# Attention items of 384 and 512 keys: the gate and the reciprocal move from a VectorE pass over the probabilities into the matrix that TensorE multiplies them by

## The chip, the cores and the metric

One NeuronCore of a Trainium2 chip runs the whole program. The metric is the device time of one execution in microseconds (us); lower is better. PE is TensorE (PEld its weight loads), DVE is VectorE, ACT is ScalarE, POOL is GpSimd, SP is SyncE.

## The reference, cut to what matters

The reference is a stack of three transformer-like blocks over 512 tokens with a model width of 1024: a gated delta net, retention, and a third block whose mixer joins an HGRN2 branch and a sparse attention (`nsa`). Each is followed by a convolutional feed-forward layer. The change touches only the last softmax part of `nsa`. It has 8 query heads of 64 channels in 2 key/value groups of 4, and three branches: over 31 compressed blocks, over selected blocks of 64 keys, and over a window of 512 keys. With 512 tokens there are only 8 blocks to select from and 16 may be selected, and the window holds every key, so that the second and third branches are both causal softmax attention over all keys, with keys and values of their own:

```
sw = einsum('bgrnqd,bgnkd->bgrnqk', qw, kwin) * scale
pw = softmax(where(mw, sw, NEG), axis=-1)
o_win = einsum('bgrnqk,bgnkd->bgrnqd', pw, vwin)
...
gates = sigmoid(g_pre)
o = gates[..., 0:1] * o_cmp + gates[..., 1:2] * o_slc + gates[..., 2:3] * o_win
```

Everything is float32.

## The kernel before, in words

The program keeps activations transposed in SBUF (channels on partitions, 512 tokens along the free axis), streams weights through a ring of three slots on SP's DMA queue, and goes through its stages one after the other. Each engine has an instruction stream written out by hand, with one semaphore per engine that counts its finished steps. A wait names the step of another engine (`at("dve", "nsa", "p", n, g)`) and an engine runs its instructions strictly in the order in which they are written.

The attention stage is `pe_nsa`, `act_nsa` and `dve_nsa`. After a part that normalizes, rotates and compresses, it loops over 36 items (`ITEMS`, L1877): for r in 0 to 3 (the head within its group) first one item of branch 0 (b = 0, compressed keys, all 512 queries at once), then for b = 1 and b = 2 four items (b, i) with i = 0 to 3. Item (b, i) holds the 128 queries of block i against the keys 0 to 128 (i + 1), and both groups g = 0 and 1. So an item with i = 2 has 384 keys and one with i = 3 has 512. `Pn` has three buffers for probabilities (queries on partitions, keys along the free axis), `PTn` two for their transposes. Banks 0, 1, 6 and 7 of PSUM hold the scores of two items, banks 2 and 3 the transposes of the two groups, banks 4 and 5 collect the output.

An item n goes through these steps.

- `scores(n)`, PE, L1942 (L1938 for b = 0): queries by keys, into a score bank. It waits until the exponentials of item n − 2 have read that bank.
- `front(n)`, DVE, L2090: adds the causal mask and finds the row maximum, in one custom instruction for each group (L2079, L2082 and L2085 for b = 0).
- `exp(n)`, ACT, L2013 (L2007 for b = 0): the exponential into `Pn`, with the row sum in `small`.
- DVE, L2113: the reciprocal of both row sums. Then L2117, one instruction for each group: the item's probabilities, in place, times reciprocal times gate; this is step "p" of (n, g). For b = 0 the lines are L2102 to L2109.
- PE, L1972: a transpose of each 128x128 block of the scaled probabilities into bank 2 + g, after step "p" of the group and after ACT's copy of the item before has read the bank.
- ACT, L2028 (L2026 for b = 0): the copy of the transposed block row from the bank to `PTn`.
- `values(n)`, PE, L1958 (L1954 for b = 0): values by transposed probabilities, added up in banks 4 and 5 over the branches. As reciprocal and gate are in the probabilities, the branches need no further scaling.

The order in each engine is what couples the items. For item n, PE does `scores(n + 2)`, the transposes of n, `values(n - 1)`. DVE does `front(n + 1)`, then waits for `exp(n)`, then the reciprocal and L2117 of n. ACT does `exp(n + 1)`, then the copies of n. In the first (b = 1) item of each r but the first, DVE also copies the finished output of r − 1 out of banks 4 and 5 into `HT` (L2136, L2137). After the last item it does so for r = 3, and the next stage's products (L267) follow.

Neither DMA nor POOL has a part in this loop. The matrix `ident` (128x128 identity) is the operand of all transposes in the program. Elsewhere, the first block's chunk code has, for each of 8 heads, four transposes of 128x128 at L996 and four plain products of 128x128 by 128 columns at L1001; four more at L1067 stream `ident` as the moving operand.

Of the kernel before, what the change touches and what calls it, by code (L numbers as in the profile page):

```python
# [12 lines left out]
P = 128  # L13
# [73 lines left out]
def program(nc, dr, out, plan):  # L87
# [3 lines left out]
    with ExitStack() as ctx:  # L91
# [7 lines left out]
        B4 = [b[:, :].rearrange("p (i c) -> p i c", c=P) for b in B]  # L99
# [22 lines left out]
        ident = sb("ident", [P, P])  # L122
# [15 lines left out]
        small = sb("small", [P, 64])  # L138
# [3 lines left out]
        def region(offset, *shape):  # L142
            size = int(np.prod(shape))
            v = arena[:, offset:offset + size]
            if len(shape) == 2:
                v = v.rearrange("p (a b) -> p a b", b=shape[1])
            if len(shape) == 3:
                v = v.rearrange("p (a b c) -> p a b c", b=shape[1], c=shape[2])
            return v
# [757 lines left out]
        o = 0  # L907
        OT_g = region(0, GH, T)
        o = GH * T
# [399 lines left out]
        o = 16 * T  # L1309
# [174 lines left out]
        o = 0  # L1484
# [6 lines left out]
        VSW = region(o, NT, 280); o += NT * 280  # L1491
# [370 lines left out]
        o = 4 * CB * NCMP  # L1862
# [3 lines left out]
        o = work  # L1866
        Pn = [region(o + m * 2 * T, 2 * NT, P) for m in range(3)]; o += 6 * T
# [1 line left out]
        tri = region(o, T); o += T  # L1869
        KCMP = region(o, 32); o += 32  # L1870
        VCMP = region(o, 2, ND); o += 2 * ND
        assert o <= 26000
        SB = ((0, 1), (6, 7))
        NORMED = [4, 0, 1, 2, 3, 6, 7]
        GAIN = {0: 0, 1: 0, 2: 0, 3: 0, 4: 1, 6: 2, 7: 3}
# [6 lines left out]
        def pe_nsa(pe):  # L1882
# [29 lines left out]
            for kv in (1, 0):  # L1912
                pe.wait_ge(act_done, at("act", "nsa", "silu", kv))
                for hc in range(2):
                    last = nc.tensor.transpose(B[6][:, (2 * kv + hc) * 2 * NCMP:(2 * kv + hc + 1) * 2 * NCMP],
                                               SIL[0:2 * NCMP, kv, hc * P:(hc + 1) * P], ident[0:2 * NCMP, 0:2 * NCMP])
# [3 lines left out]
            for g in range(NG):  # L1920
# [3 lines left out]
                for hc in range(2):  # L1924
                    last = nc.tensor.matmul(B[3][0:NCMP, g * ND:(g + 1) * ND], HID[:, 2 + hc, blk], w2c[:, 1, hc, :],
                                            start=(hc == 0), stop=(hc == 1))
# [37 lines left out]
            for n, (r, b, i) in enumerate(ITEMS):  # L1964
                if n + 2 < len(ITEMS):
                    scores(n + 2)
                for g in range(NG):
                    pe.wait_ge(dve_done, at("dve", "nsa", "p", n, g))
                    if n:
                        pe.wait_ge(act_done, at("act", "nsa", "pt", n - 1, g))  # L1970
                    for j in range(NT if b == 0 else i + 1):
                        last = nc.tensor.transpose(B4[2 + g][:, j, :], Pn[n % 3][:, 4 * g + j, :], ident[:, :])  # L1972
                    last.then_inc(pe_done, PE.tick("nsa", "pt", n, g))
                if n:
                    values(n - 1)
# [56 lines left out]
        def dve_nsa(dve):  # L2032
            begin(dve, "dve", "nsa")

            def step(ins):

                ins.then_inc(dve_done, DV.tick())
                dve.wait_ge(dve_done, DV.n)

            def blocks_of(kv):  # L2040
                for g in range(NG):
                    for a in range(2):

                        tok = NX[half(g), 4 + kv, a * CS:a * CS + NCMP * CS].rearrange("p (n l) -> p l n", l=CS)
                        dst = XP[half(g), kv, a * CS:(a + 1) * CS, g * NCMP:(g + 1) * NCMP]
                        pos = pecmp[half(g), kv, a * CS:(a + 1) * CS].rearrange("p (l o) -> p l o", o=1).to_broadcast([ND, CS, NCMP])
                        ins = nc.vector.tensor_tensor(dst, tok, pos, ALU.add)  # L2047
                ins.then_inc(dve_done, DV.tick("nsa", "blocks", kv))

            blocks_of(1)  # L2050
            for n, c in enumerate(NORMED):
                dve.wait_ge(act_done, at("act", "nsa", "std", n))
                nc.vector.scalar_tensor_tensor(out=NX[:, c, :], in0=NX[:, c, :], scalar=gvec[:, 8 + GAIN[c]:9 + GAIN[c]], in1=rsn[n % 2],
                                               op0=ALU.mult, op1=ALU.mult).then_inc(dve_done, DV.tick("nsa", "normed", n))
                dve.wait_ge(pe_done, at("pe", "nsa", "rot", n))
                nc.vector.tensor_tensor(tan, B[2 + n % 2][:, :], SINF, ALU.mult).then_inc(dve_done, DV.tick())
                step(nc.vector.tensor_tensor(NX[:, c, :], NX[:, c, :], COSF, ALU.mult))
                nc.vector.tensor_tensor(NX[:, c, :], NX[:, c, :], tan, ALU.add).then_inc(dve_done, DV.tick("nsa", "rotated", n))
                dve.wait_ge(dve_done, DV.n)
                if c == 4:  # L2060
                    blocks_of(0)
            for m in range(3):

                nc.vector.memset(Pn[m][:, :, :], 0.0).then_inc(dve_done, DV.tick())
            nc.vector.memset(tri, 0.0).then_inc(dve_done, DV.tick())
            dve.wait_ge(dve_done, DV.n)
            step(nc.vector.tensor_copy(tri[:, 3 * P:4 * P], causal[:, 2, :]))
            cm = cmask[:, :, 0:NCMP]
            valid = cmask[:, :, 31:32].rearrange("p i o -> p (i o)")

            def front(n):

                r, b, i = ITEMS[n]
                dve.wait_ge(pe_done, at("pe", "nsa", "score", n))
                if b == 0:
                    S = [B4[SB[n % 2][g]][:, :, 0:NCMP] for g in range(NG)]
                    m4 = [small[:, 24 + 4 * g:28 + 4 * g] for g in range(NG)]
                    for g in range(NG):
                        ins = nc.vector.tensor_tensor(S[g], S[g], cm, ALU.add)  # L2079
                    step(ins)  # L2080
                    for g in range(NG):
                        ins = nc.vector.reduce_max(m4[g], S[g], AX)  # L2082
                    step(ins)
                    for g in range(NG):
                        nc.vector.tensor_tensor(S[g], S[g], m4[g].rearrange("p (i o) -> p i o", o=1).to_broadcast([P, NT, NCMP]), ALU.subtract)\  # L2085
                            .then_inc(dve_done, DV.tick("nsa", "max", n, g))
                else:
                    for g in range(NG):
                        S, c = B[SB[n % 2][g]], 2 * (n % 2) + g
                        nc.vector.tensor_tensor_reduce(out=S[:, 0:(i + 1) * P], in0=S[:, 0:(i + 1) * P], in1=tri[:, (3 - i) * P:4 * P],  # L2090
                                                       scale=-SCALE, scalar=3e38, op0=ALU.add, op1=ALU.min,
                                                       accum_out=small[:, 20 + c:21 + c]).then_inc(dve_done, DV.tick("nsa", "max", n, g))

            front(0)
            for n, (r, b, i) in enumerate(ITEMS):
                if n + 1 < len(ITEMS):
                    front(n + 1)
                dve.wait_ge(act_done, at("act", "nsa", "exp", n, 1))
                if b == 0:
                    Pc = Pn[n % 3][:, :, 0:NCMP]  # L2100
                    s8 = small[:, 32:40]
                    step(nc.vector.reduce_sum(s8, Pc, AX))  # L2102
                    step(nc.vector.reciprocal(s8, s8))
                    for g in range(NG):
                        s4 = s8[:, 4 * g:4 * g + 4]
                        step(nc.vector.tensor_tensor(s4, s4, valid, ALU.mult))
                        step(nc.vector.tensor_tensor(s4, s4, VSW[:, :, 256 + 3 * (NG * 2 * g + r)], ALU.mult))
                        w4 = s4.rearrange("p (i o) -> p i o", o=1).to_broadcast([P, NT, NCMP])
                        nc.vector.tensor_tensor(Pc[:, 4 * g:4 * g + 4, :], Pc[:, 4 * g:4 * g + 4, :], w4, ALU.mult)\  # L2109
                            .then_inc(dve_done, DV.tick("nsa", "p", n, g))  # L2110
                else:
                    c = 40 + 2 * (n % 2)
                    step(nc.vector.reciprocal(small[:, c:c + 2], small[:, c:c + 2]))  # L2113
                    for g in range(NG):
                        head = NG * 2 * g + r
                        p = Pn[n % 3][:, 4 * g:4 * g + i + 1, :].rearrange("p j c -> p (j c)")
                        nc.vector.tensor_scalar(p, p, small[:, c + g:c + g + 1], VSW[:, i, 256 + 3 * head + b:257 + 3 * head + b],  # L2117
                                                ALU.mult, ALU.mult).then_inc(dve_done, DV.tick("nsa", "p", n, g))
                if b == 1 and i == 0 and r:
                    dve_o(dve, r - 1)  # L2120
            dve_o(dve, 3)
            DV.mark("end", "nsa")
# [357 lines left out]
```

## Time and profile before

| what | value |
|---|---|
| median of 3 runs | 3007.68 us (3004.35 to 3011.74) |
| the profiled execution's own time | 3000.66 us |
| its span, first to last instruction | 2998.6 us, 29328 instructions |
| PE busy | 2813.1 us, 94% |
| DVE busy | 1547.3 us, 52% |
| ACT busy | 640.8 us, 21% |
| POOL busy | 149.6 us, 5% |
| mean granted TensorE clock | 0.969 of full speed |

A busy time is the union of an engine's instructions; records of PE overlap each other, since matmuls are pipelined. A line number is that of the kernel's source, so all instructions of a program line fall into a group. The "idle before" of a group is the time its engine had nothing to do just before the group's instructions, and the arrow names what ended it. The attention loop described above runs from about 2437 to 2530 us of the span.

### The profile page before, as it was taken

The page shows a single profiled execution, that of the slowest core. Times are in us where ns is not written, and L with a number is a line of the kernel's source. Part 1 is how long each engine was busy: PE and PEld are TensorE (multiplying, and loading weights), DVE is VectorE, ACT ScalarE, POOL GpSimd, SP SyncE. Part 2 cuts the span into 40 slices and gives each one's busy share as a digit, 9 for nine tenths or more (in the row PEclk, how much of TensorE's full clock was granted, in tenths as well). Part 3 has the DMA queues.
Part 4 walks back from the last instruction along what each step waited for, and adds up shares of the span by engine and source line. Part 5 has one row for each costly group of instructions (what it writes and reads, how often), then busy time and mean ns, then how long its engine had stood idle before and what let it go on. Part 6 is the DMA issues. An engine that isn't in the chain of part 4 may idle for free. (4 is left out here: it accounts for less than half of the span.)

```text
span 2998.6 us, 29328 instructions
## 1 busy us (share of the span) xinstructions
PE 2813.1 (94%) x11724; PEld 1964.9 (66%) x11724; DVE 1547.3 (52%) x2740; ACT 640.8 (21%) x1124; POOL 149.6 (5%) x118
## 2 busy tenths in 40 slices
PE   6999999988999999999989899999699899999999
PEld 5566666656888884444434688888245445588888
DVE  4555555546777542112211677764646566566652
ACT  0211122102111002111110211100635465222200
POOL 0000000001000001000000100000122200000000
PEclk9999999899999999999989999999899999999999
DMA  7111121112444331111112244433011130222121
GB/s 306 39 57 56 60 91 75 57 41 85 164 166 157 149 124 65 58 60 60 65 51 84 84 169 165 155 134 123 32 56 44 57 113 1 82 88 85 67 97 48
DMA packets 24486, 274.95 MB, mean 92 GB/s; under 512 B 3480, under 2 KB 4376, under 8 KB 7072
## 3 DMA queue, kind: packets, MB, share of 16 engines
q1 hardware_dynamic: 19440, 266.45, 24.0%
q10 hardware_dynamic: 4912, 6.63, 0.7%
q8 instruction: 94, 1.54, 0.2%
q14 instruction: 40, 0.33, 0.0%
HBM read 270.97 MB, written 2.10 MB: 91 GB/s over the span
## 5 line engine op out<-in xcount | busy, mean ns | idle before, releaser
L323 PE MATMUL bank<-HT,ring 128*128 128x256 f32 x1056 | 256.6, 388 | 21.0 <-ACT HT L671 12.7
L939 PE MATMUL bank<-HT,ring 128*128 128x512 f32 x512 | 261.0, 640 | 0.0
L323 PE MATMUL bank<-arena 128*128 128x256 f32 x1056 | 249.5, 379 | 0.0
L323 PE MATMUL bank<-arena,ring 128*128 128x256 f32 x1056 | 249.5, 379 | 0.0
L323 PEld LDWEIGHTS bank<-HT,ring 128*128 128x128 f32 x1056 | 203.3, 194 | 52.2 <-issue 24.2
L323 PEld LDWEIGHTS bank<-arena 128*128 128x128 f32 x1056 | 200.6, 190 | 27.3
L323 PEld LDWEIGHTS bank<-arena,ring 128*128 128x128 f32 x1056 | 200.6, 190 | 27.3
L400 PE MATMUL bank<-arena,ring 128*128 128x256 f32 x936 | 207.5, 380 | 5.7 <-ACT arena L470 3.8
L267 PE MATMUL bank<-arena,ring 128*128 128x512 f32 x448 | 199.8, 606 | 11.0 <-issue 9.6
L400 PEld LDWEIGHTS bank<-arena,ring 128*128 128x128 f32 x936 | 177.0, 190 | 31.1 <-ACT arena L470 5.1
L244 DVE SCALAR_TENSOR_TENSOR arena<-ring,evec,arena 128x512 f32<-128x512 f32 x224 | 167.3, 747 | 3.8
L267 PEld LDWEIGHTS bank<-arena,ring 128*128 128x128 f32 x448 | 87.0, 195 | 122.1 <-issue 122.1
L860 ACT ACTIVATE arena<-bank,ffc 128x512 f32<-128x512 f32 x66 | 51.3, 777 | 471.3 <-DVE bank L788 471.3
L1535 PE MATMUL bank<-HT,ring 128*128 128x512 f32 x320 | 147.6, 598 | 4.3 <-ACT HT L699 4.3
L939 PEld LDWEIGHTS bank<-HT,ring 128*128 128x128 f32 x512 | 95.4, 205 | 79.1 <-issue 79.1
L323 PE MATMUL bank<-HT,arena 128*128 128x256 f32 x528 | 126.5, 382 | 0.9 <-DVE arena L838 0.8
L1355 PE MATMUL bank<-ring,HT 128*128 128x512 f32 x256 | 114.7, 608 | 8.2 <-ACT arena L660 8.2
L1336 PE MATMUL bank<-HT,ring 128*128 128x512 f32 x256 | 113.6, 605 | 6.3 <-ACT HT L671 6.3
L400 PE MATMUL bank<-arena 128*128 128x256 f32 x528 | 116.4, 379 | 0.0
L323 PEld LDWEIGHTS bank<-HT,arena 128*128 128x128 f32 x528 | 98.6, 190 | 19.3 <-DVE arena L838 6.5
L1369 PE MATMUL bank<-HT,ring 128*128 128x512 f32 x256 | 110.5, 592 | 0.0
L605 DVE SCALAR_TENSOR_TENSOR XT<-bank,mod,XT 128x512 f32<-128x512 f32 x24 | 18.0, 751 | 178.3 <-PE bank L267 178.3
(396 smaller groups left out, 4014.2 us busy)
## 6 DMA issues: line engine op xcount, KB each, us to landing
ring<-w_ada SPq DMA_DIRECT2D x33, 2048.0 KB, 8.0
ring<-w_up SPq DMA_DIRECT2D x33, 2048.0 KB, 7.8
ring<-w_down SPq DMA_DIRECT2D x24, 1408.0 KB, 6.0
ring<-w_gdn SPq DMA_DIRECT2D x8, 2048.0 KB, 12.4
ring<-w_ret_qk SPq DMA_DIRECT2D x4, 2048.0 KB, 7.9
ring<-w_ret_v SPq DMA_DIRECT2D x4, 2048.0 KB, 7.8
ring<-w_ret_g SPq DMA_DIRECT2D x4, 2048.0 KB, 7.9
ring<-w_ret_out SPq DMA_DIRECT2D x4, 2048.0 KB, 7.8
```

The lines of the kernel that those rows point to most:

```text
L244: ins = nc.vector.scalar_tensor_tensor(out=acc, in0=w[:, :, k, :], scalar=evec[:, e, k:k + 1], in1=acc, op0=ALU.mult, op1=ALU.add)
L267: last = nc.tensor.matmul(bank[:, :], w[:, n % per_load, k, :], src(k), start=(k == 0), stop=(k == kc - 1))
L323: last = nc.tensor.matmul(out_, w[:, k, :], x[:, k, :], start=(first and k == 0), stop=(k == 3), skip_group_check=not first)
L400: last = nc.tensor.matmul(out_, w[:, k, :], x(k), start=(first and k == 0), stop=(k == KH2 - 1), skip_group_check=not first)
L605: nc.vector.scalar_tensor_tensor(out=XT[:, n, :], in0=B[n % 2][:, :], scalar=g[:, i, gate + n:gate + n + 1], in1=XT[:, n, :], op0=ALU.mult ...
L860: nc.scalar.activation(ffn_y[:, j % 2, :], B[j % 2][:, :], ACT.Identity, scale=ffc[:, i, j, 0, 2:3], bias=ffc[:, i, j, 0, 3:4])\
L939: last = nc.tensor.matmul(B[u % 2][:, :], w[:, u, k, :], HT[:, k, :], start=(k == 0), stop=(k == KC - 1))
L1336: last = nc.tensor.matmul(B[X + u][:, :], w[:, u, k, :], HT[:, k, :], start=(k == 0), stop=(k == KC - 1))
L1355: last = nc.tensor.matmul(B[Y + i][:, :], HT[:, k, i * P:(i + 1) * P], w[:, k, :], start=(k == 0), stop=(k == KC - 1))
L1369: last = nc.tensor.matmul(B[Y + u][:, :], w[:, u, k, :], HT[:, k, :], start=(k == 0), stop=(k == KC - 1))
L1535: last = nc.tensor.matmul(bank[:, :], w[:, u, k, :], HT[:, k, :], start=(k == 0), stop=(k == KC - 1))
```

## The change

In items of 384 and 512 keys (b > 0, i >= 2) L2117 no longer multiplies the probabilities. It multiplies the identity by reciprocal and gate, which gives a diagonal matrix of 128x128, into one of six new buffers `scale_n` (three items by two groups). PE then multiplies each block of the unscaled probabilities by this diagonal, with a plain `matmul` in place of the `transpose` with the identity. The result is the same scaled, transposed block in the same bank. The other items (b = 0 and i < 2) stay as they were. Waits and semaphore steps stay the same, and so does the number of instructions in the program's text.

```
         VCMP = region(o, 2, ND); o += 2 * ND
-        assert o <= 26000
+        scale_n = [region(o + m * P, P) for m in range(6)]; o += 6 * P
+        assert o <= 26000, o
...
                     for j in range(NT if b == 0 else i + 1):
-                        last = nc.tensor.transpose(B4[2 + g][:, j, :], Pn[n % 3][:, 4 * g + j, :], ident[:, :])
+                        if b == 0 or i < 2:
+                            last = nc.tensor.transpose(B4[2 + g][:, j, :], Pn[n % 3][:, 4 * g + j, :], ident[:, :])
+                        else:
+                            last = nc.tensor.matmul(B4[2 + g][:, j, :], Pn[n % 3][:, 4 * g + j, :], scale_n[2 * (n % 3) + g], start=True, stop=True)
                     last.then_inc(pe_done, PE.tick("nsa", "pt", n, g))
...
                     for g in range(NG):
                         head = NG * 2 * g + r
-                        p = Pn[n % 3][:, 4 * g:4 * g + i + 1, :].rearrange("p j c -> p (j c)")
-                        nc.vector.tensor_scalar(p, p, small[:, c + g:c + g + 1], VSW[:, i, 256 + 3 * head + b:257 + 3 * head + b],
+                        if i < 2:
+                            p = q = Pn[n % 3][:, 4 * g:4 * g + i + 1, :].rearrange("p j c -> p (j c)")
+                        else:
+                            p, q = scale_n[2 * (n % 3) + g], ident[:, :]
+                        nc.vector.tensor_scalar(p, q, small[:, c + g:c + g + 1], VSW[:, i, 256 + 3 * head + b:257 + 3 * head + b],
                                                 ALU.mult, ALU.mult).then_inc(dve_done, DV.tick("nsa", "p", n, g))
```

## Rows read from the trace of the kernel before

**Rows 1.** The page's busy line of PE, whole span: busy us, share, instructions.

```profile
PE 2813.1 (94%) x11724; PEld 1964.9 (66%) x11724; DVE 1547.3 (52%) x2740; ACT 640.8 (21%) x1124; POOL 149.6 (5%) x118
```

**Rows 2.** Windows, the attention loop: length, busy us (instructions) of each engine, clock, DMA.

```profile
2437.00:2530.00 93.00, 83.90 (x704) 52.01 (x705) 74.00 (x283) 63.82 (x208) 0.00 (x0) 0.98 0.01 1
```

**Rows 3.** Waits from 2437 to 2530: who for whom, us in total, times, longest.

```profile
ACT arena L2028 <- PE bank L1972: 18.4, 31, 1.1
...
PE bank L1972 <- DVE arena L2117: 5.3, 8, 1.1
```

**Rows 4.** Timeline around item (1, 2) of r = 2: start, us, engine, line, idle.

```profile
2487.72 1.13 PE L1942 MATMUL bank<-arena 64*128 64x512 f32 x4
...
2490.36 0.87 DVE L2117 TENSOR_SCALAR arena<-arena,small 128x384 f32<-128x384 f32 x2
...
2490.89 0.94 PE L1972 MATMUL bank<-ident,arena 128*128 128x128 f32 x6 [0.67 <-DVE arena L2117]
```

**Rows 5.** Timeline around items (2, 2) and (2, 3) of r = 1; last row: r = 2.

```profile
2476.90 1.08 PE L1938 MATMUL bank<-arena 64*128 64x31 f32 x16
...
2477.53 0.87 DVE L2117 TENSOR_SCALAR arena<-arena,small 128x384 f32<-128x384 f32 x2
...
2478.06 0.94 PE L1972 MATMUL bank<-ident,arena 128*128 128x128 f32 x6
...
2478.31 0.48 DVE L2079 TENSOR_TENSOR bank<-bank,cmask 128x124 f32<-128x124 f32 x2
...
2479.93 1.00 DVE L2117 TENSOR_SCALAR arena<-arena,small 128x512 f32<-128x512 f32 x2
...
2480.53 1.11 PE L1972 MATMUL bank<-ident,arena 128*128 128x128 f32 x8 [0.52 <-DVE arena L2117]
...
2502.69 1.11 PE L1972 MATMUL bank<-ident,arena 128*128 128x128 f32 x8 [0.52 <-DVE arena L2117]
```

**Rows 6.** Timeline, the last two items of the loop (r = 3).

```profile
2522.39 0.93 PE L1972 MATMUL bank<-ident,arena 128*128 128x128 f32 x6 [1.10 <-DVE arena L2117]
...
2523.85 1.09 PE L1972 MATMUL bank<-ident,arena 128*128 128x128 f32 x8
2524.60 1.09 ACT L2028 ACTIVATE arena<-bank 128x512 f32<-128x512 f32 x2 [0.69 <-PE bank L1972]
...
2524.87 1.96 PE L1958 MATMUL bank<-arena 128*64 128x128 f32 x28
```

**Rows 7.** Lines L996, L1001 and L1067: records, ns min/median/max, first and last start.

```profile
L996 PEld LDWEIGHTS bank<-ident,arena x32: 140/141/144, 115.7 to 599.3; 128*128 128x128 f32 x32
L996 PE MATMUL bank<-ident,arena x32: 272/273/273, 115.8 to 599.4; 128*128 128x128 f32 x32
...
L1001 PEld LDWEIGHTS bank<-arena x64: 186/192/193, 116.3 to 600.4; 128*128 128x128 f32 x64
L1001 PE MATMUL bank<-arena x64: 275/275/348, 116.4 to 600.5; 128*128 128x128 f32 x64
...
L1067 PE MATMUL bank<-ident,rqk x64: 275/275/561, 170.6 to 638.6; 128*128 128x128 f32 x64
```

**Rows 8.** Timeline of PE, a batch of plain 128x128 products (L1014, first block).

```profile
125.59 1.05 PE L1014 MATMUL bank<-arena 128*128 128x128 f32 x8
```

**Rows 9.** Timeline, the transposes of item (1, 0) of r = 2.

```profile
2485.90 0.44 PE L1972 MATMUL bank<-ident,arena 128*128 128x128 f32 x2
```

**Rows 10.** Lines by form, L2117: count, busy us, mean ns, idle before.

```profile
L2117 DVE TENSOR_SCALAR arena<-arena,small 128x512 f32<-128x512 f32 x16 | 8.0, 544 | 0.3
L2117 DVE TENSOR_SCALAR arena<-arena,small 128x384 f32<-128x384 f32 x16 | 6.9, 476 | 0.3
L2117 DVE TENSOR_SCALAR arena<-arena,small 128x128 f32<-128x128 f32 x16 | 4.8, 344 | 0.3
```

**Rows 11.** Timeline: the copies of item (1, 3), r = 2, and PE's reading.

```profile
2493.74 1.08 ACT L2028 ACTIVATE arena<-bank 128x512 f32<-128x512 f32 x2 [0.63 <-PE bank L1972]
...
2496.03 1.09 PE L1958 MATMUL bank<-arena 128*64 128x128 f32 x16
```

## The prediction

> **What bounds the kernel now.** The busy line of the page first [rows 1]: TensorE (PE) is busy for 94% of the span. That is a mean over stages, so the second view is the one of windows, for the attention loop alone (2437 to 2530 us) [rows 2]: PE is busy 83.9 of 93.0 us, VectorE (DVE) 74.0, ScalarE (ACT) 63.8. PE has 9 us to spare there, and the third view, the waits [rows 3], says where: 5.3 us in 8 waits of the transposes at L1972 for the DVE multiplication at L2117; the rest lies at the loop's two ends and in crumbs. So the loop is PE's, save for two places in each of the four rounds (a round is the nine items of one r).
>
> The timeline shows both. **Place A**, item (1, 2), 384 keys [rows 4]: PE ends scores of 512 columns at 2488.85; DVE can reduce these scores (L2090) only then, before the reciprocal and L2117, which starts at 2490.36 and releases the transposes at 2490.89. PE had 0.67 us of nothing. **Place B**, item (2, 3), 512 keys [rows 5]: after L2117 of item (2, 2) DVE makes the next round's front (from L2079 at 2478.31), then the reciprocal, and L2117 at 2479.93 releases PE at 2480.53, after 0.52 us of nothing. Between these places PE's instructions stand end to end. In the last round B has no next front before it, so that its 512-key item waits for nothing, and its 384-key item (2, 2) waits 1.10 us in the manner of A [rows 6]. That makes 4 + 3 + 1 = 8 waits.
>
> **What the change costs PE.** The items of 384 and 512 keys have 3 and 4 blocks for each of 2 groups: 6 and 8 products, twice in each round, 4 × 2 × 14 = 112 in all. A transpose is one record: L996 has 8 heads × 4 = 32 in the program and 32 in the trace. A plain fp32 product of the same shape, L1001, also 8 × 4 in the program, has 64 records [rows 7]: two passes each. L1067, with the identity streamed as the changed line streams a diagonal, has 64 for its 32 too. Eight plain records in a row last 1.05 us [rows 8] and one lasts 0.275 [rows 7], so they start (1.05 − 0.275) / 7 = 0.111 us apart. Eight transposes in two groups last 1.09 us [rows 6], two in two groups 0.44 [rows 9]: six more in 0.65 us, 0.108 each. So a product costs 2 × 0.111 − 0.108 = 0.113 us more. All 112: **12.7 us** of added PE time; an item of 384 keys gets 0.68 us, one of 512 keys 0.90.
>
> The nearest rows bound this price. Below: one record after all, nothing more. Above: if the longer weight load (0.192 against 0.141 us, L1001 and L996 [rows 7]) stood in the open for both records, 2 × 0.05 = 0.10 more, 0.213 in all and 24 us for the 112. L1001's loads are no less long, and the eight records of L1014, which are of the same shape, still start 0.111 apart, so I take 0.113.
>
> **A rule against this change.** What the trace has is one record against two, 0.108 against 0.222 us [rows 7, 8]. The Trainium skill (TensorE: Matmul & The Clock Gate, section Terms) says of the transpose mode that it is "4× faster for FP32". The rows here give a factor of two. By the rule each product would cost 3 × 0.108 = 0.32 us more, 36 us in all; this is an estimate from that page, taken up below as a rival.
>
> **What it gives DVE.** L2117 shrinks from 384 or 512 columns to 128: 0.476 and 0.544 us to 0.344 [rows 10]. Two for each item, that is 0.26 and 0.40 us less, and 8 × 0.66 = 5.3 us of DVE's time. Only what stands ahead of PE's eight waits can be had back. The wait of A ends with the first L2117 alone: 0.476 − 0.344 = 0.13 us. B's has a pair of 384 before the front and one L2117 of 512: 0.26 + 0.20 = 0.46 us. Instructions, semaphores and their order stay as they are; nothing is added to ACT or to a DMA queue. The exponentials (L2013) still end before L2117 starts and are not made earlier. The copies by ACT (L2028) start later with the products that they wait for; the products by V that read them (L1958) are those of the item before, one PE turn later, and have 1.2 us of room even for 512 keys: the copies end at 2494.82, PE reads them at 2496.03 [rows 11]. That cover is whole for all items except the last of the loop.
>
> **The sum, place by place.** A, four times: PE starts 0.13 us earlier and works 0.68 longer: +0.55. Item (1, 3) behind it, four times: PE arrives later than DVE already, all of it counts: +0.90. B, three times: item (2, 2) starts at 2478.06, PE having ended at 2477.98, so it can gain 0.08 only, and takes 0.68 more: +0.60. This eats B's idle 0.52 [rows 5]; DVE's release moves from 2480.53 to 2480.07, so PE is now the late one, and item (2, 3) starts 0.08 us later. Then its own +0.90. That makes 0.98. Three rounds: 3 × (0.55 + 0.90 + 0.98) = 7.3 us. Last round: A 0.55, (1, 3) 0.90, (2, 2) 0.55 (1.10 us wait for DVE, shortened by 0.13), and the end. There PE does the products by V of (2, 2), 12 records from 2524.87 on, and then the 16 of (2, 3), which wait for ACT's copies, done at 2525.69; all end at 2526.83 [rows 6]. Twelve of 28 records in 1.96 us are 0.84, so (2, 2) is through at 2525.71. With 0.90 us more the transposing products, which ended at 2524.94, end at 2525.84 and the second copy (half of the 1.09 us) some 0.6 later, while PE gets through with (2, 2) at 2526.61: +0.75 by the one, +0.90 by the other, I take 0.85. DVE's two copies into HT (L2136, L2137) and the next stage hang on that. Last round 2.85. Together **10.1 us slower**.
>
> The profiled execution took 3000.66 us (span 2998.6 and 2.1 around it). That is 7.0 below the median of the runs, 3007.68, and 3.7 below the lowest, 3004.35. Its durations make the difference of 10.1; I put it on the median: 3007.68 + 10.1 = **3017.8 us**, a factor of 1.0034. A measurement of this kernel can tell about 0.3% from no change, 9.0 us, and the forecast lies just over it.
>
> **Rivals.**
> *One record each.* The diagonal's products might go at the transposes' pace, so that only DVE's gain is left: 4 × 0.13 + 3 × 0.46 + 0.13 = 2.0 us faster, 3005.7. The point from which it decides: a round's A and B give 0.13 + 0.46 = 0.59 us and have 28 products, so below 0.59 / 28 = 0.021 us more for a product the change doesn't lose. L1001 and L1067 speak against it with two records for each. 3%.
> *More cover than I see.* The longer turns of PE let DVE and ACT run ahead, and the crumbs of idle time go as well as B's: 12.7 less all 5.3 us of the eight waits, 7.4 us, 3015.1, and within 0.3%. Against it: at A PE waits for a chain that begins with its own scores, so A's 0.67 us can't be eaten. 12%.
> *Nothing covered.* Behind longer turns ACT's copies or an exponential come late, and B's 0.52 us is only moved: 12.7 us and no gain, 3020.4. For it: ACT waits 18.4 us in 31 waits for L1972 [rows 3], so it follows PE closely; against it, the room of 1.2 us above. 10%.
> *Four times.* A pace of 0.43 us for a product: 112 × 0.32 = 36 us, less DVE's 0.65 at A and what B covers, some 2.5 in all: 33 us, 3041. The page's estimate above is what this would be. The 64 records of L1001 speak against it. 2%.
> *The forecast*, 73%.
>
> Within the forecast the bound at 9.0 us is 1.1 us away, and the scatter of the runs shown is ±3.7: 6 in 10 of it fall above, the others within. Slower 0.44 + 0.09 + 0.02 + a little of the second rival, 0.58; faster 0.02, for the first rival's 2.0 us are themselves within 0.3%; the rest, 0.40, within. The range takes in 7.4 and 12.7 us with some 3 us of scatter on either side: 3011.5 to 3023.5.
>
> **What would show it.** In the changed trace L1972 has 80 records of transposes and 224 of plain products, weight loads near 0.19 us; its busy time is up by 12 to 13 us. A batch for 512 keys is 16 records in about 2.0 us. L2117 has only rows of 128 and 256 columns, 48 of 128. A round takes 22.16 us now (2502.69 less 2480.53 [rows 5]) and should take 24.6 (22.16 + 2.43). A's wait should be 0.54 us, B's none. The loop should end 10 us later and every other stage be as it was. The forecast is wrong if L1972 has 192 records, if a wait for ACT's copies or its exponentials stands before a PE batch in this loop, or if B still waits.

## The result, and the profile after

The changed kernel took 3011.33 us (median of 20 runs, 3005.49 to 3015.79) against 3005.12 (20 runs, 3001.65 to 3013.89): a ratio of **1.0018, 95% interval 1.0011 to 1.0024**, 5.4 us slower (3.3 to 7.2); the two medians are 6.2 us apart. The forecast was 10.1 us, a ratio of 1.0034, with 3017.8 us and a range that began at 3011.5. The direction was right, the size was not, and the median fell just below the range. The base was off too: the forecast added to 3007.68 us, the median of three runs, and twenty runs of the kernel before have 3005.12. The profiled execution took 3006.45 us, 5.8 above that of before. All figures here are of fast executions; two slow ones of the fifth set, of 4608.9 and 4921.8 us at mean clocks of 0.60 and 0.57, are left out.

The loop itself did what was forecast. It is measured from one end to the other by two PE instructions that both kernels have: the first product by V of branch 0 in round 0 (L1954, now L1955), and the first product of the next stage (L267). Timeline, before:

```profile
2442.38 1.07 PE L1954 MATMUL bank<-arena 31*64 31x512 f32 x4
...
2528.48 3.67 PE L267 MATMUL bank<-arena,ring 128*128 128x512 f32 x8 [1.65 <-issue]
```

and after:

```profile
2437.73 1.07 PE L1955 MATMUL bank<-arena 31*64 31x512 f32 x4
...
2533.83 3.67 PE L267 MATMUL bank<-arena,ring 128*128 128x512 f32 x8 [1.65 <-issue]
```

That is 86.10 us before and 96.10 after: **+10.0 us**. But the loop begins 4.65 us earlier, after 2.4 ms of a program that the change doesn't touch. From L267 to the end of the span it is 470.1 us before and 470.6 after. So in this pair of traces 4.65 of the 10.0 are missing ahead of the loop.

Windows of just this stretch, before and then after (columns as in [rows 2]):

```profile
2442.38:2528.48 86.10, 77.75 (x683) 48.42 (x683) 70.03 (x263) 60.58 (x197) 0.00 (x0) 1.00 0.01 2
```

```profile
2437.73:2533.83 96.10, 90.23 (x795) 62.88 (x795) 65.35 (x263) 62.04 (x196) 0.00 (x0) 1.00 0.01 2
```

PE has 112 records more and 12.5 us more busy time, DVE 4.7 us less; PE's idle time goes from 8.35 to 5.87 us. The clock is at its full 2.4 GHz level in both.

Lines by form of after, for [rows 10] and L1972:

```profile
L1976 PE MATMUL bank<-arena 128*128 128x128 f32 x224 | 29.3, 282 | 3.1 <-DVE arena L2124 3.1
L1976 PEld LDWEIGHTS bank<-arena 128*128 128x128 f32 x224 | 26.2, 191 | 6.2 <-DVE arena L2124 4.1 <-issue 1.5
...
L2124 DVE TENSOR_SCALAR arena<-ident,small,arena 128x128 f32<-128x128 f32 x32 | 9.6, 344 | 0.6
```

The 112 products are 224 records, as L1001 said. Their weight loads take 191 ns, and 16 records still take 2.05 us, so that the loads are hidden. PE's waits for DVE's scaling went from 5.3 us in 8 to 3.1 in 5. This is place A of after, in the round of [rows 4], and then place B, in the round of [rows 5]:

```profile
2487.82 1.13 PE L1943 MATMUL bank<-arena 64*128 64x512 f32 x4
...
2490.46 0.60 DVE L2124 TENSOR_SCALAR arena<-ident,small,arena 128x128 f32<-128x128 f32 x2
...
2490.86 1.60 PE L1976 MATMUL bank<-arena 128*128 128x128 f32 x12 [0.54 <-DVE arena L2124]
```

```profile
2476.12 1.08 PE L1939 MATMUL bank<-arena 64*128 64x31 f32 x16
...
2477.15 1.60 PE L1976 MATMUL bank<-arena 128*128 128x128 f32 x12
...
2478.88 0.60 DVE L2124 TENSOR_SCALAR arena<-ident,small,arena 128x128 f32<-128x128 f32 x2
...
2479.27 0.49 PE L1943 MATMUL bank<-arena 64*128 64x128 f32 x4
2479.69 2.05 PE L1976 MATMUL bank<-arena 128*128 128x128 f32 x16
```

A keeps a wait of 0.54 us (0.67 less 0.13). At B there is none: DVE has made both diagonals by 2479.48, PE arrives at 2479.69. A batch for 512 keys is 16 records in 2.05 us.

### The profile page after: what moved, and what is told of

It reads as the page before. It is cut to its first block and busy times, and to the rows that moved or that the text cites. A ratio compares the mean times of both kernels' runs of the same rounds, so it can differ in the third digit from the quotient of the medians.

```text
span 3004.4 us, 29552 instructions
## 1 busy us (share of the span) xinstructions
PE 2830.0 (94%) x11836; PEld 1988.9 (66%) x11836; DVE 1543.0 (51%) x2740; ACT 642.4 (21%) x1124; POOL 149.6 (5%) x118
## 5 line engine op out<-in xcount | busy, mean ns | idle before, releaser
L323 PE MATMUL bank<-HT,ring 128*128 128x256 f32 x1056 | 258.0, 390 | 20.0 <-ACT HT L671 12.7
L323 PEld LDWEIGHTS bank<-arena 128*128 128x128 f32 x1056 | 200.6, 190 | 27.3
L267 PE MATMUL bank<-arena,ring 128*128 128x512 f32 x448 | 198.5, 603 | 11.0 <-issue 9.6
L267 PEld LDWEIGHTS bank<-arena,ring 128*128 128x128 f32 x448 | 86.6, 194 | 121.4 <-issue 121.4
L1535 PE MATMUL bank<-HT,ring 128*128 128x512 f32 x320 | 148.7, 602 | 4.3 <-ACT HT L699 4.3
L1336 PE MATMUL bank<-HT,ring 128*128 128x512 f32 x256 | 113.5, 605 | 6.3 <-ACT HT L671 6.3
L400 PEld LDWEIGHTS bank<-arena 128*128 128x128 f32 x528 | 100.3, 190 | 13.6
```

The costliest lines, as they stand in the source:

```text
L267: last = nc.tensor.matmul(bank[:, :], w[:, n % per_load, k, :], src(k), start=(k == 0), stop=(k == kc - 1))
L323: last = nc.tensor.matmul(out_, w[:, k, :], x[:, k, :], start=(first and k == 0), stop=(k == 3), skip_group_check=not first)
L400: last = nc.tensor.matmul(out_, w[:, k, :], x(k), start=(first and k == 0), stop=(k == KH2 - 1), skip_group_check=not first)
L1336: last = nc.tensor.matmul(B[X + u][:, :], w[:, u, k, :], HT[:, k, :], start=(k == 0), stop=(k == KC - 1))
L1535: last = nc.tensor.matmul(bank[:, :], w[:, u, k, :], HT[:, k, :], start=(k == 0), stop=(k == KC - 1))
```

## The experiments

The question became where the missing 4 to 5 us are. There were three theories: **loop plus scatter** (the change costs its 10.0, and the first set of timings drew low), **outside** (something in the changed program makes the rest shorter in every execution), **cheaper product** (executions other than the traced ones pay less for a plain product). The kernels below also test the pieces of the sum. "Loop" is always the stretch defined above. A number of us behind a ratio is the ratio's part of the time of before in that set. Timings taken together, against the same runs of the kernel before, are called a set; the first set is the result above.

### Second set: the change taken apart

**null**, the kernel before with the buffers named and unused:

```
+        scale_n = [region(o + m * P, P) for m in range(6)]; o += 6 * P
```

> The kernel before with the six new buffers named but not used: its instructions are those of before. All theories: loop 86.1 us from the first products by V of branch 0 in round 0 to the first product of the next stage, as before, and a ratio of 1.000. What is wanted is the scatter: if two equal programs come out more than 2 us apart, the 5.4 us measured for the change (with 10.0 in the loop of the two traces) can be scatter; if they stay within 1 us, something outside the loop or in unprofiled runs has to explain the other 4.6 us.

Loop 86.11 us, ratio 1.0001 (0.9991 to 1.0010), +0.3 us. The medians, however, are 2.4 us apart the other way (3002.15 against 3004.58), so this set alone doesn't decide between scatter and a cause outside the loop.

**pe_alone**, only PE's part:

```
-                        last = nc.tensor.transpose(B4[2 + g][:, j, :], Pn[n % 3][:, 4 * g + j, :], ident[:, :])
+                        if b == 0 or i < 2:
+                            last = nc.tensor.transpose(...)
+                        else:
+                            last = nc.tensor.matmul(B4[2 + g][:, j, :], Pn[n % 3][:, 4 * g + j, :], ident[:, :], start=True, stop=True)
```

> Only PE's part: items of 384 and 512 keys are multiplied by the identity with a plain product, DVE still scales 384 and 512 columns. Theory 'loop': 224 records, A 4 x (0.68 + 0.90), B 3 x (0.09 + 0.90) since its idle 0.52 covers most of the 0.68, last items 0.68 + 0.85, in all +10.8 us in the loop and +10.8 in the median. Theory 'outside': +10.8 in the loop, and the median is some 4.6 us short of it, +6, as for the change. Theory 'cheaper unprofiled': half of it in the median, +5.4, and in the change-and-double kernel too.

Loop 97.17 us, +11.1; ratio 1.0035 (1.0022 to 1.0047), +10.5 us. Nearly all of the loop's time arrives in the whole here (6.6 to 14.1 by the interval), which speaks against a product that is cheaper by half.

**dve_alone**, only DVE's part (reciprocal and gate are left out of the items' results):

```
-                        if b == 0 or i < 2:
-                            last = nc.tensor.transpose(...)
-                        else:
-                            last = nc.tensor.matmul(..., scale_n[2 * (n % 3) + g], start=True, stop=True)
+                        last = nc.tensor.transpose(...)
```

(against the changed kernel)

> Only DVE's part: the diagonals are made (128 columns), but PE transposes the probabilities of these items with the identity as before, so reciprocal and gate are left out of their result. Theory 'loop': A 4 x -0.13, B 3 x -0.46, last -0.13: -2.0 us in the loop and in the median. Theory 'outside': -2.0 in the loop, -6 to -7 in the median. Theory 'cheaper unprofiled': -1 to -2.

Loop 83.68 us, −2.4; ratio 0.9990 (0.9981 to 0.9999), −3.0 us. The extra 4.6 us that "outside" asks for are not there. The parts are −2.4 and +11.1, together +8.7, where the change has +10.0: B's idle time is used once, either by DVE's gain or by PE's longer item.

**twice**, each diagonal product issued twice:

```
+                            nc.tensor.matmul(B4[2 + g][:, j, :], Pn[n % 3][:, 4 * g + j, :], scale_n[2 * (n % 3) + g], start=True, stop=True)
                             last = nc.tensor.matmul(B4[2 + g][:, j, :], Pn[n % 3][:, 4 * g + j, :], scale_n[2 * (n % 3) + g], start=True, stop=True)
```

> The changed kernel with each of the 112 diagonal products issued twice: 224 more records at 0.111 us. Theory 'loop': 96.1 + 24.9 = 121 us of loop, +35 us in the median against before. Theory 'outside': +35 in the loop, +30 in the median. Theory 'cheaper unprofiled' (a plain record costs half of what the trace shows): about +18 in the median.

Loop 121.13 us. The 112 added products cost 25.03, 0.2235 each, which is the forecast's 2 × 0.111. Ratio 1.0105 (1.0091 to 1.0119), +31.6 us of the 35.0 in the loop. That is far from 18; the gap of 3.4 has an interval of ±4, so it is not clear of nothing.

### Third set: the change again, one part more, and two changes of order

**after2**, the changed kernel.

> The changed kernel again, on this chip. Its own trace has the loop 10.0 us longer and the part before the loop 4.7 us shorter than before's, though that part is the same program. If the 4.7 us is scatter of single executions: loop 96.1 again, the part before the loop anywhere within 2449 to 2456, and over this set of runs a ratio between 1.0025 and 1.004. If something in the changed program lowers the rest in every execution: loop 96.1, ratio 1.0015 to 1.002 again.

Loop 96.11, ratio 1.0031 (1.0019 to 1.0043), +9.3 us. In this set nothing is clearly missing. Its part before the loop ends at 2437.46 us. (The expectations count that part from some 11 us before the first instruction: the 2442.38 of before is 2453.7 there, and the 2437.73 of after 2449.0. Counted so, `after2` has 2448.7, just under the 2449 to 2456 that were named.)

**all_diag**, the diagonal for all items with b > 0:

```
-                        if b == 0 or i < 2:
+                        if b == 0:
...
-                        if i < 2:
+                        if b == 0:
```

> The diagonal for every item with b > 0, so for 128 and 256 keys too: 48 more products, 5.4 us of PE time. In the loop: in rounds 0 to 2 the 0.45 of item (1, 1) goes into A's wait of 0.54, item (2, 1) pays 0.45 and the two of 128 keys 0.23 each; in the last round (2, 1) too is covered, by a wait of 0.96. Loop 96.1 + 3.2 = 99.3 us. Theory 'loop plus scatter': median 13.2 above before. Theory 'outside': 8.6 to 9 above.

Loop 98.64 us, 2.5 more than the change where 3.2 were expected; ratio 1.0049 (1.0037 to 1.0061), +14.7 us. For the shorter items the sum was 0.7 us too high: PE's waits for L2124 went from 3.1 us in 5 to 0.5 in 1, so that more of the added 5.4 us was covered than the 2.2 of the sum. Nothing is won by it.

**early_after**, the changed kernel with DVE's order changed for items (1, 2), (2, 2) and (2, 3) of each round, so at A, at B and at one item that doesn't wait:

```
+                early = b and (i == 2 or (b, i) == (2, 3))
-                if n + 1 < len(ITEMS):
+                if n + 1 < len(ITEMS) and not early:
                     front(n + 1)
...
+                if n + 1 < len(ITEMS) and early:
+                    front(n + 1)
```

(the second after the reciprocal and the scaling of n)

> The changed kernel with DVE's order changed at A and B: reciprocal and diagonal of item n ahead of the front of n + 1. A's wait of 0.54 goes, four times, the last 0.96 too, of which 0.3 comes back before the last item: loop 96.1 - 2.8 = 93.3 us. If the later front delays the exponentials of the 512-key item by more than PE's longer turn covers, a new wait for L2124 stands before the item of 512 keys and the loop gains less than 1 us.

Loop 92.81 us, −3.3 against the change. No wait of PE for L2124 is left in the loop. This is its PE timeline at A, with no idle time printed:

```profile
2486.99 0.49 PE L1943 MATMUL bank<-arena 64*128 64x128 f32 x4
2487.41 1.60 PE L1976 MATMUL bank<-arena 128*128 128x128 f32 x12
```

Ratio 1.0023 (1.0013 to 1.0033), +6.9 us for +6.7 in the loop.

**values_first**, the kernel before with PE's order changed for the same three items of each round, so in the last round for (2, 3) too, which did not wait:

```
+                first = b and (i == 2 or (b, i) == (2, 3))
+                if first:
+                    values(n - 1)
                 for g in range(NG):
                     pe.wait_ge(dve_done, at("dve", "nsa", "p", n, g))
...
-                if n:
+                if n and not first:
                     values(n - 1)
```

> The kernel before, with PE's order changed at A and B alone: the products by V of item n - 1 ahead of the transposes of n, so that they fill the wait for DVE. 8 waits, of which 4 x 0.59, 3 x 0.52 and 0.59 are filled: loop 86.1 - 4.5 = 81.6 us, ratio 0.9985. If PE's waits there are not what the loop's time hangs on, or DVE's next front comes late in turn, the loop stays within 1 us of 86.1.

This was a miss: loop 84.45 us, −1.65 instead of −4.5; ratio 0.9998 (0.9989 to 1.0007). This is a line of its waits (who for whom, us in total, times, longest), and then the timeline at B:

```profile
PE bank L1958 <- ACT arena L2031: 2.5, 6, 0.8
```

```profile
2492.50 0.88 PE L1958 MATMUL bank<-arena 128*64 128x128 f32 x12 [0.27 <-ACT arena L2031]
...
2495.17 0.42 PEld L1975 LDWEIGHTS bank<-ident,arena 128*128 128x128 f32 x4 [0.54 <-DVE arena L2112]
2495.17 1.26 PE L1975 MATMUL bank<-ident,arena 128*128 128x128 f32 x8
```

PE's 5.3 us of waits for the scaling became 0.2, but the products by V now come early enough to wait for ACT's copies themselves: 2.5 us in 6 waits that the kernel before doesn't have. Three of them are the 0.27 us at B; the other three, 0.22, 0.63 and 0.80 us, are in the last round, where they and the 0.21 for DVE are more than the 1.10 us that was to be filled. And now that PE is early, the next round's branch-0 item, which has the longest chain on DVE, holds it up: its eight transposes last 1.26 us in place of 1.09, the length of any eight before ([rows 6]), with a gap for L2112 between the groups. So most of what was filled came back as other waits.

### Fourth set: scatter, and a better order

**after3** and **after4** are the changed kernel, **null2** the instructions of before.

> The changed kernel a third time. Its loop has been 96.10 and 96.11 us against 86.10 and 86.11. Theory 'loop plus scatter': this set's ratio lies between 1.0025 and 1.004, since the first set's 1.0018 drew low and the second's was 1.0031. Theory 'outside': 1.0015 to 1.002. A ratio between the two leaves it open.

> The changed kernel a fourth time, a copy of the third, so that the spread between two equal kernels of one set is seen: theory 'loop plus scatter' as for the third, and the two within 3 us of each other. The part before the loop of the two traces within 2445 to 2456 us, not at one value.

> The instructions of the kernel before again: loop 86.1, ratio within 0.999 and 1.001; the part before the loop somewhere within 2445 to 2456 us, which no theory of the loop touches.

Loops 96.11, 96.11 and 86.11 us. Ratios 1.0032 (1.0019 to 1.0044), 1.0032 (1.0019 to 1.0045) and 1.0007 (0.9998 to 1.0016). Counted as in the expectations, the part before the loop ends at 2451.4, 2450.6 and 2458.0 us; the last, of the unchanged instructions, lies above the 2445 to 2456 that were named.

**combo**, the kernel before with PE's order changed at A and the last round's second wait, and DVE's at B:

```
+                first = i == 2 and (b == 1 or r == 3)
...
+                early = (b, i) == (2, 3)
```

(with the lines of `values_first` and `early_after` that use them)

> The kernel before with two changes of order: at A, and in the last round at its second wait, PE does the products by V of the item before ahead of the transposes (0.59 us of the wait filled each time); at B DVE makes reciprocal and scaling of the 512-key item ahead of the next round's front (0.52 us of wait gone). Loop 86.1 - 5 x 0.59 - 3 x 0.5 = 81.6 us. If the front of the next round comes late for it, a wait for L2112 stands before its branch-0 transposes and the loop keeps 83.1.

Loop 83.96 us, −2.1; ratio **0.9987 (0.9978 to 0.9996)**, −3.9 us. The second outcome that was named came, though by less (83.1 was said), with a wait of 0.48 us for the branch-0 scaling:

```profile
2476.61 1.09 PE L1975 MATMUL bank<-ident,arena 128*128 128x128 f32 x8
2477.63 0.88 PE L1958 MATMUL bank<-arena 128*64 128x128 f32 x12
2478.44 0.70 PE L1942 MATMUL bank<-arena 64*128 64x256 f32 x4
2479.62 1.25 PE L1975 MATMUL bank<-ident,arena 128*128 128x128 f32 x8 [0.48 <-DVE arena L2113]
```

B's 512-key item now starts right after the scores, and what was won there is lost two batches later. What is left is what was won at A and in the last round.

### Fifth set: the theories against each other

> The changed kernel in a further set. Loop 96.1. Theory 'loop plus scatter': ratio 1.0025 to 1.004, as in the two sets before (1.0031, 1.0032, 1.0032). Theory 'outside': 1.0015 to 1.002, as in the first set.

> A copy of the same, for more executions in this set: as above; both theories have its part before the loop vary by some us from trace to trace, and only 'outside' has it lie 4 to 5 us below that of the unchanged instructions in the same set.

> The unchanged instructions, in the same set: ratio 0.999 to 1.001, loop 86.1. Its part before the loop is compared with those of the two changed kernels of this set: equal within the scatter of 2.5 us by 'loop plus scatter', 4 to 5 us longer by 'outside'.

The loops take 96.09, 96.08 and 86.09 us, and yet the ratios are 1.0006 (0.9996 to 1.0016), 1.0008 (0.9996 to 1.0019) and 0.9993 (0.9983 to 1.0003): +1.8, +2.4 and −2.1 us. So "loop plus scatter" fails in its simple form: seven or eight microseconds are missing in this set, beyond the intervals, and the unchanged instructions of `null3` came out low too. In the traces of this set nothing is missing: the loop begins at 2439.34 us in null3, at 2440.50 in after5 and 2439.29 in after6.

> The two changes of order once more: loop 83.96 as before, 2.1 us under 86.1, so a ratio of 0.9993 by the loop alone; 0.9987 was measured. If the order gives what the loop shows and no more, this set lies at 0.9990 to 0.9996.

**combo2**: loop 83.91, ratio 0.9988 (0.9978 to 0.9997), a second time below 1, just under the 0.9990 to 0.9996 that were expected. That is −3.6 us, 1.4 more than the loop gives (2.2); against `null3` of the same set, −2.1, it is only 1.5 faster.

### Sixth set: does the gap grow with the products?

**four**, each diagonal product issued four times (two more lines like that of `twice`), and **after7**, the changed kernel.

> The changed kernel with each diagonal product issued four times: 672 records more than the changed kernel. Loop 96.1 + 3 x 25.0 = 171 us, 85.0 above before. The doubled kernel had 35.0 more in the loop and 31.5 in the mean of its executions; the changed one 10.0 and between 2 and 9.6. If executions other than the traced ones pay some tenth less for a plain product, the gap grows with the products: 75 to 78 in the median. If the gap is between loadings of a program and has nothing to do with the products, it stays within 0 to 8 us: 77 to 85, and most likely 81 to 84.

> The changed kernel in one more set. Loop 96.1. Sets so far: 1.0018, 1.0031, 1.0032 and 1.0006. If sets differ by the loading of the program, this one lies anywhere between 1.000 and 1.0035; a value near 1.0033 is what the loop alone gives.

**four**: loop 171.14 us, +85.0; ratio 1.0283 (1.0268 to 1.0298), +85 us (80.4 to 89.4). The 75 to 78 of a product that is a tenth cheaper in executions other than the traced ones lie outside this interval, and "cheaper product" falls; a gap that doesn't grow with the products, of up to 4.6 us, would still fit. **after7**: loop 96.10, ratio 1.0024 (1.0015 to 1.0034), +7.2 us.

## Why the prediction was right or wrong

**The price of a product: right.** Forecast 0.222 us for two records. Measured 0.2235 in `twice` (25.03 / 112) and 0.2233 in `four` ((171.14 − 96.10) / 336). By the Trainium skill's "4× faster for FP32" for the transpose mode (TensorE: Matmul & The Clock Gate, section Terms) it would be 0.43, an estimate from that page. The runs disagree and decide: they give a factor of 2.07 over the 0.108 of a transpose.

**The loop, place by place: right.** A round grew from 22.16 to 24.54 us, 2.38 where the sum had 2.43. From the last round's first product by V of branch 0 to L267 it grew by 2.88 (19.60 to 22.48), where the sum had 2.85. A's wait went to 0.54 and the last round's from 1.10 to 0.96 as forecast:

```profile
2526.23 1.60 PE L1976 MATMUL bank<-arena 128*128 128x128 f32 x12 [0.96 <-DVE arena L2124]
...
2528.35 2.05 PE L1976 MATMUL bank<-arena 128*128 128x128 f32 x16
...
2530.33 1.85 PE L1959 MATMUL bank<-arena 128*64 128x128 f32 x28
```

At B PE was to reach the 512-key item 0.08 us later; counted from the branch-0 scores (3.63 us from L1938 to L1972 in [rows 5], 3.57 from L1939 to L1976 above) it is 0.06 earlier. A batch for 512 keys in turn adds 0.96 us rather than 0.90 from its start to that of the next batch (1.02 in [rows 6], 1.98 here), twice in a round. The two errors nearly cancel. The 28 records at the end, 1.96 us before [rows 6], now run through in 1.85 without the wait for ACT. The prediction's signs came as named (80 transposes, 224 plain records, a round of 24.54 us, B without a wait) save one that it had read wrongly: it took any wait for ACT's copies before a PE batch for a sign of error, and said that between A and B PE's instructions stand end to end. There is such a wait, of 0.37 us, before the first products by V of branch 0 in rounds 1 to 3, and it is in both kernels alike (in round 2 at 2486.71 us of before and at 2486.81 of after), so that it changes nothing in the difference.

**The step that failed** is the one that put the difference of the loop on the median: "Its durations make the difference of 10.1; I put it on the median". It has two parts, and both failed. The base, 3007.68 us, is the median of three runs, and twenty runs gave 3005.12: 2.6 of the 6.5 us by which 3017.8 was missed. On the base of 3005.12 the same sum gives 3015.2 and a range from about 3009, which holds the 3011.33. The difference takes the 2.9 ms outside the loop to be the same in both kernels, in the mean of a set: the other 3.9 us. What the sets showed (the means are of each set's executions, of before and then of the kernel named):

| kernel | loop against 86.1 | whole, us against before (interval) | mean of before | mean of the kernel |
|---|---|---|---|---|
| first set | +10.0 | +5.4 (3.3 to 7.2) | 3005.7 | 3011.2 |
| after2 | +10.0 | +9.3 (5.7 to 12.9) | 3001.7 | 3010.3 |
| after3, after4 | +10.0, +10.0 | +9.6, +9.6 (5.7 to 13.5) | 3000.8 | 3010.1, 3010.1 |
| after5, after6 | +10.0, +10.0 | +1.8, +2.4 (−1.2 to 5.7) | 3006.6 | 3008.6, 3010.0 |
| after7 | +10.0 | +7.2 (4.5 to 10.2) | 3001.8 | 3009.1 |
| null, null2, null3 | 0.0, 0.0, 0.0 | +0.3, +2.1, −2.1 | 3004.4, 3000.8, 3006.6 | 3004.0, 3002.3, 3005.1 |

The whole is always less than the loop, by 0.4 to 8.2 us; the plain mean of the seven is +6.5. The changed kernel's own mean hardly moved (3008.6 to 3011.2); that of the kernel before did (3000.8 to 3006.6), and where it was high the difference is small. The loop's part repeats to 0.04 us. The rest doesn't repeat: the same program up to the loop arrives there at very different times. In two traces of one kernel, combo and combo2, the loop's first product (L1954) starts at 2440.07 and at 2449.08 us.

Over the seven traces of the changed kernel this start lies between 2437.46 and 2442.01 us, mean 2439.6; over the four of the unchanged instructions between 2439.34 and 2446.36, mean 2442.1. The difference of 2.6 us has the sign of what is missing and three quarters of its mean size, but combo's two traces alone are 9 us apart. The other kernels have the same instructions up to the loop, and `four`, built on the changed kernel, begins it at 2446.63, `values_first` at 2434.56. Over all twenty traces the twelve with the plain products have a mean of 2440.3 and the eight without 2442.2: 1.8 us, with single traces 14.5 apart.

**What is settled and what stays open.** Settled: the change costs 10.0 us where it acts, and executions other than the traced ones pay for its products too (`four`). Open: whether the rest of the changed kernel is really some 3.5 us shorter in the mean, or whether seven measurements in five sets drew low. Kernels of equal instructions differed by up to 2.1 us from the kernel before in a set, while the difference of the changed one ranged over 7.8. Most of that range comes from the kernel before's own mean, which moved by 5.8 from set to set. Against the copies of the unchanged instructions in the same set the means differ by 7.8 (`after3` and `after4` against `null2`) and by 4.2 (`after5` and `after6` against `null3`). Nothing was found in the program that would explain a shorter rest: up to the loop the instructions are the same. Two rivals were not tested by themselves. One is how a program was loaded for a set, named in an expectation. The other is the chip: the sets of `after2` and `after7` ran on one, that of `after3` on a second and that of `after5` on a third, and the smallest differences and the slowest mean of the kernel before are those of the third. For the first set the chip is not on record, and one chip alone had that mean at 3004.4, 3001.7 and 3001.8 in three sets.

**The rivals.** "One record each" fell with the 224 records, "four times" with 0.2235 us for a product. "More cover than I see" named 7.4 us and "nothing covered" 12.7; both are refused by the loop's 10.0, though the whole of the first set lay below the first of them. The forecast's own split, 6 in 10 above 0.3% and the rest within, was for scatter of the runs shown. It had no allowance for a base from three runs or for offsets between sets, and the range's lower end, some 3 us of scatter below 7.4, was too near. That the result lies only 0.2 us outside the range is no merit of the number: a smaller difference and a lower base added up.

## What to carry to other kernels

An fp32 transpose on TensorE is one record and a plain fp32 product of the same shape two: folding a scale into the transposing matrix doubles PE's time for it, and pays only where the shorter scaling takes more than 0.113 us for each block out of PE's waits. Here it took 0.13 us out of A's wait, for six blocks. Where PE is the bound of a stage, a wait of PE is better won by order than by work: `combo`, with the order changed at eight places of the loop and no work taken away, has a loop 2.1 and 2.2 us shorter than that of before in its two traces (0.9987 and 0.9988 of the whole, by the same intervals that were too narrow for a comparison of sets). Even so, `values_first` shows that a filled wait can come back on another engine. And when the change is a few tenths of a per cent, measure the stage in the trace between two instructions that both kernels have; of the whole, take several sets before a gap is given a cause, and look at the base's own mean in each of them.

## What the runs showed that was not expected

The stretch of one stage at full clock repeated to 0.04 us over eleven traces (86.09 to 86.11, 96.08 to 96.11), on runs whose whole scattered by 10 us and more. Nearly all of that scatter lies ahead of the loop: from L267 to the end of the span nineteen of the twenty traces have 469.6 to 470.8 us, and `values_first` 471.6, while the loop's start ranges from 2434.56 to 2449.08. In `combo` and `combo2` it builds up over the whole way: L1336 first starts at 1134.0 and 1139.5 us, L1535 at 2124.2 and 2132.5, the loop at 2440.07 and 2449.08. It goes with the clock: of the changed kernel's twenty executions in the first set, nine had a mean granted clock of 0.967 or more and a median of 3008.4 us, eleven had less and a median of 3014.4. That doesn't explain the offsets between sets: the kernel before had a mean clock of 0.9671 in the set where it took 3004.4 us and of 0.9665 where it took 3001.7. The windows of the first 640 us show one stretch where the clock is not full: PE's granted clock is 0.93 to 0.94 there, between its two levels (1.2 and 2.4 GHz) in the mean, against 1.00 in the loop (0.94 in the trace of `null3`, 0.93 in that of `after5`).

And the intervals of single sets (±0.1%) did not hold across sets: 1.0006 (up to 1.0016) and 1.0031 (from 1.0019) were measured for the same kernel.
